# Eighty transposes of the identity into unread banks, ahead of five waits of the mixing

## The reference, cut to what matters

```python
h   = rms_norm(x, norm_mix)
aq, ak, av, mq, mk, mv, mo, gt = split(h @ w_in)
att = diff_attention(aq, ak, av, lam)          # 4 heads
mem = mlstm_mixer(mq, mk, mv, mo, gt)          # 4 heads, forward and backward
x   = x + concat(norm(att), norm(mem)) @ w_out
x   = x + peer(rms_norm(x, norm_ffn), ...)     # q = xn @ wq, two scores of 128 keys per head, top 16, experts
x   = x + (p @ ple_w_proj) * sigmoid(rms_norm(x, norm_ple) @ ple_w_gate)
y   = rms_norm(x, norm_final)
```

## Time and profile before

| | us |
|---|---|
| median of 3 runs | 2435.35 |
| lowest and highest of them | 2428.57, 2440.18 |
| the profiled execution, its own time | 2437.25 |
| its span (first to last instruction) | 2435.5 |
| TensorE busy in the span | 2268.7 |

### The profile page before, as it was taken

One profiled execution on the slowest core, in us unless ns is written; L12 is line 12 of the kernel. 1 busy time (PEld: TensorE's weight loads), 2 busy tenths in 40 slices (PEclk: granted clock), 3 DMA queues, 4 the chain that ended last, 5 costly groups with the idle time before them and its releaser, 6 DMA issues.

```text
span 2435.5 us, 27329 instructions
## 1 busy us (share of the span) xinstructions
PE 2268.7 (93%) x9992; PEld 1127.4 (46%) x9992; DVE 1796.6 (74%) x3557; ACT 788.1 (32%) x1222; POOL 776.7 (32%) x617
## 2 busy tenths in 40 slices
PE   7989998998879989999999999959999999999897
PEld 5445743445435434445545454424444444444443
DVE  3350087678656588999999997768888898888373
ACT  4241112115221124454444454423323332333203
POOL 0000100211437601232333254435444545444150
PEclk9988999999889999999999999979999999999998
DMA  5313412223569945878878799999999999999261
GB/s 173 137 69 120 166 69 87 97 77 121 166 241 346 329 153 186 334 253 309 309 284 296 266 356 357 368 396 386 389 388 387 388 389 385 385 380 346 98 232 53
DMA packets 244053, 625.41 MB, mean 257 GB/s; under 512 B 18640, under 2 KB 84560, under 8 KB 232656
## 3 DMA queue, kind: packets, MB, share of 16 engines
q1 hardware_dynamic: 146544, 275.49, 32.2%
q0 software_dynamic: 75776, 274.76, 31.0%
q10 hardware_dynamic: 21600, 73.41, 7.6%
HBM read 547.05 MB, written 76.55 MB: 256 GB/s over the span
## 4 chain that ended last, share of the span: by engine, by line
PE 59%; DVE 25%; DMA 7%; POOL 3%; ACT 3%; issue 2%; SPq 1%; DVEq 0%; ACTq 0%
PE ps L1025 27%; PE ps L739 18%; PE ps L980 5%; DVE arena L1689 4%; DVE arena L1586 4%; DMA arena<-peer_u,pk 3%; POOL arena L676 3%; PE ps L840 3%; DVE arena L1769 2%; DMA arena<-peer_v,pk 1%; DVE pk L1612 1%; DVE pk L1609 1%; DVE arena L1765 1%; DVE arena L1766 1%; SPq L583 1%
## 5 line engine op out<-in xcount | busy, mean ns | idle before, releaser
L980 PE MATMUL ps<-arena 128*128 128x512 bf16 x3072 | 684.7, 383 | 22.2 <-DVE arena L1586 18.7
L1025 PE MATMUL ps<-arena 128*128 128x512 bf16 x3072 | 665.3, 380 | 20.3 <-DVE arena L1795 20.3
L676 POOL DMA_INDIRECT arena<-peer_u,pk x256 | 367.2, 1434 | 642.7 <-DVE pk L1689 580.7
L739 PE MATMUL ps<-arena 128*128 128x512 f32 (+2 forms) x1552 | 554.7, 515 | 6.8 <-ACT arena L1074 2.8
L676 POOL DMA_INDIRECT arena<-peer_v,pk x256 | 362.6, 1416 | 434.6 <-DVE arena L1704 399.3
L1025 PEld LDWEIGHTS ps<-arena 128*128 128x128 bf16 x3072 | 300.4, 98 | 385.2 <-issue 23.6
L980 PEld LDWEIGHTS ps<-arena 128*128 128x128 bf16 x3072 | 298.5, 98 | 379.7 <-DVE arena L1586 24.0
L739 PEld LDWEIGHTS ps<-arena 128*128 128x128 f32 x1552 | 287.0, 194 | 255.6 <-issue 238.4
L1704 DVE SCALAR_TENSOR_TENSOR arena<-arena,pk 128x1024 f32<-128x1024 f32 x256 | 328.3, 1282 | 77.5 <-DMA arena<-peer_v,pk 69.9
L1689 DVE CUSTOM_DVE_ANT_0 arena<-arena 128x1024 f32<-128x1024 f32 x256 | 308.2, 1219 | 104.2 <-DMA arena<-peer_u,pk 103.2
L1345 ACT ACTIVATE arena<-arena 128x1024 bf16<-128x1024 f32 x128 | 134.7, 1054 | 447.7 <-PE ps L1025 269.0
(11 more groups left out here) (179 smaller groups left out, 1607.9 us busy)
## 6 DMA issues: line engine op xcount, KB each, us to landing
arena<-uT SPq DMA_DIRECT2D x128, 512.0 KB, 5.3
arena<-peer_v SPq DMA_DIRECT2D x64, 1024.0 KB, 15.6
scr_gelu<-arena ACTq DMA_DIRECT2D x128, 256.0 KB, 5.4
scr_gates<-arena ACTq DMA_DIRECT2D x16, 2048.0 KB, 10.8
arena<-scr_gelu SPq DMA_DIRECT2D x64, 512.0 KB, 11.8
arena<-scr_gates SPq DMA_DIRECT2D x32, 1024.0 KB, 16.3
arena<-w_in SPq DMA_DIRECT2D x14, 2048.0 KB, 8.0
arena<-peer_wq SPq DMA_DIRECT2D x8, 2048.0 KB, 11.3
```

The lines of the kernel that those rows point to most:

```text
L676: g.indirect_dma_start(out=u_rows[place], out_offset=None, in_=peer_u if r < NS * NSLOT else peer_v, in_offset=bass.IndirectOffsetOnAxis(a ...
L739: mm = nc.tensor.matmul(out, lhs(c), rhs(c), start=(c == 0), stop=(c == n - 1))
L980: mm = nc.tensor.matmul(ps[:, n % 2, :], w[n % 4][:, c, :], x[:, c, :], start=(c == 0 and w is uh and x is xh), stop=(c == DC - 1 and w is ...
L1025: mm = nc.tensor.matmul(ps[:, 2 * t + half, :], abf[b][:, pa, k, t * P:(t + 1) * P], vbf[b][:, pv, k, half * 512:half * 512 + 512], start= ...
```

## The change

A function `idle_products(bank, n)` issues n transposes of the identity against itself into the first 128 columns of a bank. They wait for nothing and raise no semaphore. It is called in five places of TensorE's list (once in `mix_out` and once in `queries`, each of which runs for B and for A, and once at the start): 24 transposes at the start, 16 at the head of `mix_out` of B and of A, 12 at the head of `queries` of B and of A, 80 in all.

```diff
+            def idle_products(bank, n):
+                for _ in range(n):
+                    nc.tensor.transpose(ps[:, bank, 0:P], ident[:], ident[:])
+
             def mix_out(s):
                 q, nt = Q[s], TILES[s]
+                idle_products(3, 16)
                 for t in range(nt):
                     pe.wait_ge(q["cnorm"], 2 * (t + 1))
...
             def queries(s):
                 q, nt = Q[s], TILES[s]
                 k = "ffn" + s
+                idle_products(7, 12)
                 norm_transposes(k, range(nt), norm_out[k])
...
             pe.wait_ge(mk, 5)
+            idle_products(7, 24)
             norm_transposes("mixB", range(2), hn)
```

## The result

| | before | after |
|---|---|---|
| median, lowest and highest of 22 runs, us | 2432.52, 2428.26, 2440.77 | 2427.29, 2417.95, 2434.42 |
| the profiled execution, its span | 2437.25, 2435.5 | 2426.09, 2424.3 |

The ratio of the times is 0.9978, with a 95% interval from 0.9968 to 0.9988: 5.2 us less, between 2.9 and 7.8. The forecast was 2.9 us less, 2432.5 us from the median of three runs, and "within 0.5%". One execution of a later kernel, `e4_middle`, took 4668.2 us, nearly twice the others, and its ratio leaves it out.

What follows compares the result with a forecast made beforehand. TensorE, busy 93% of the span, was taken as the bound, the change acting only through its clock. Gains of 1.1 (mixing B), 1.1 (mixing A) and 0.7 us (queries B) took 2435.35 to 2432.5 us, range 2423 to 2440.5.

Steps and rivals of the forecast that it cites:

- Cost of the products, 0: At all five places the products lie in TensorE's idle time: 0 on the path, bounds 0 and 0.35 us.
- Rival 3: Products writing the same columns don't overlap and overrun the waits: 6.7 us slower, 2442.1 us, chance 0.05.
- The ceilings: Most a kept clock could give: mixing B 3.6, queries B 2.9, mixing A 5.2, start 3.8, queries A 2.35 us.
- Start and queries of A, 0: At least 3.5 us and 9.7 us stay empty behind the products there, so no gain: 0.
- One sign: At the start, the stream begins at 16.6 us and is slow to about 21, as before.
- Mixings and queries of B, 2.9 us: Gain from a clock kept longer: mixing B 1.1, mixing A 1.1, queries of B 0.7 us.
- The term for the queries of B (0.7): Ahead of the queries of B the wait shrinks from 3.38 to 1.7 us; one time in four 2.9 us.
- The mechanism in B: In the mixing of B the clock's fall moves from before the first tile into the tiles: 0.7 us, plus 0.4.
- It reaches the end: Gains in mixing B and queries B move all that follows; late rows in A could not take back 1.1 us.
- The rule on transposes: Skill's rule that the full clock doesn't engage for transposes: sum 0, 2435.4 us; the trace's rise at 710.3 us disagrees.
- Rival 2: Clock kept at the start, both mixings and the queries of B: 15.5 us gained, 2419.9 us, chance 0.06.

Runs made afterwards that it cites:

- e4_middle: The change with only the products of both mixing outputs and the queries of B (16, 16, 12): 2427.58 us, ratio 0.9976 against the kernel before.
- e3_ends: The change with only the 24 products at the start and 12 ahead of the queries of A: 2433.55 us, ratio 1.0002 against the kernel before.
- e8_tiles: The change plus 12 products behind each tile's eight transposes in both mixing outputs: 2423.55 us, ratio 0.9964 against the kernel before.
- e1_narrow: The change with each of the 80 products replaced by a one-column product of the identity, no transpose: 2431.43 us, ratio 0.9995 against the kernel before.
- e5_over: The change with 80 products instead of 16 ahead of each mixing output, 60 instead of 12 at the queries of B: ratio 0.9996 against the kernel before.

## Why the prediction was right

- **Cost of the products, 0.** Right. The five waits keep 1.8 to 5.5 us of idle time, and L1421 and L1576 still release TensorE. A product costs 1.91 us / 16 = 0.12 us at 2.4 GHz with its tail, under the bound of 0.1375. Rival 3 did not come: products that write the same columns ran at the same pace as others.
- **The ceilings.** Right: 3.6, 2.9, 5.2 and 3.8 us were predicted, 3.57, 2.86, 5.15 and 3.52 measured when everything was filled.
- **Start and queries of A, 0.** Right, by `e3_ends`, whose interval leaves room for 2.4 us at most. At the start the clock even rose early, and the empty stretch behind took it back, as the step said. One sign failed: the start's stream was to be slow to about 21 us as before, and in the change's profiles it was fast throughout, as it was in `e4_middle` without products.
- **Mixings and queries of B, 2.9 us.** Right in sign and place, small in size: the median moved by 5.2 us, with 2.9 at the very edge of the interval. The term was put together from chances (one in five, one in four, one in eight) that no row gave, so that it came within a factor of two is in part luck. The forecast of 2432.5 us also stood on a median of three runs that was 2.8 us above that of 22. In the three profiles with these products (the change twice, `e4_middle`) B gained 3.6, 0.2 and 0.2, A 0, 0.6 and 2.7, the queries of B nothing: 2.4 us on average. The term for the queries of B (0.7) seems too high (`e8_tiles`, with the same 12 products there, gained 0.6), and where the other 3 us of the median come from three profiles can't tell. It stays open.
- **The mechanism in B.** The step had one picture, a clock that is high and falls later. The second profile and `e4_middle` fit it: the fall moved into the first tile. The 3.6 us of the first profile came another way that the step did not have: the clock had fallen before the products, rose among them at 173.1 us and was still up at the stream.
- **It reaches the end.** Right: the filled waits gave 16.0 us at the end for 15.1 at the four places, to which the queries of A add up to 2.35. The interval of the ratio, 11.7 to 20.2 us, is too wide to say more than that most of it arrives.
- **The rule on transposes.** The row at 710.3 us was the better guide. In the change the clock rose among transposes of the identity, at 5.9 and at 173.1 us; in `e1_narrow`, with one-column products in their place, it did not. The Trainium skill, TensorE: Matmul & The Clock Gate, Part 4: PE-mode transpose, says that the full clock doesn't engage for transposes. For the float32 transposes of this kernel the runs disagree with it, by these rises and by 5 us to 26 us gained with nothing but transposes.
- **Rival 2**, the clock kept nearly everywhere, did not come: in the first profile one place of four. It needed the filling of the tiles as well, as its "against" had said.

## What to carry to other kernels

Where one engine's wait is short, ask first which clock the work behind it runs at: the same row at two clocks gives the ceiling. Work that nobody reads was worth issuing here when it was full 128-column transposes (with one column it brought nothing), ended before the wait did, and covered the thin stretch behind the wait too: 16 us, where the change with its waits covered by half got 5, and from a different place in each profile. Products past the end of a wait delay the work behind it by their full time: in `e5_over` 12.5 us of delay ate what the clock gave.

## What the runs showed that I had not expected

- The scatter between executions of the kernel after goes with the clock. In its 22 runs, those with a mean granted clock of 0.966 and 0.967 took 2427.4 to 2434.4 us, those with 0.973 and 0.974 took 2418.0 to 2421.6 (correlation of time and clock -0.89). In the kernel before it does so far less: its clocks lie between 0.967 and 0.971 over 29 runs, the times between 2425.8 and 2440.7 us, correlation -0.43. What the rest of that kernel's scatter comes from no run here shows.
- The start is itself a draw: without any product `project` began at 26.43, 26.19 and (`e4_middle`) 23.80 us, with 24 products between 23.75 and 25.80.
- 32 one-column instructions at 1.2 GHz took 6.83 us, 0.21 us each, as long as a transpose of 128 columns at that clock (eight of L911 in 1.94 us, 0.24 each with the tail): the busy time alone doesn't tell the two apart.
